# Attention outputs: leaving the output bank by ScalarE, divided by VectorE two heads at a time

## The chip, the cores and the metric

The kernel runs on one core of a Trainium2 chip. The metric is device time in microseconds (us) of one execution. A core has five engines with queues of their own: TensorE (PE in the profile, its weight loads as PEld), VectorE (DVE), ScalarE (ACT), GpSimd (POOL) and SyncE (SP, which here only issues DMAs). Each engine executes its list in order; they wait for one another through semaphores. Matmuls write PSUM, which has 8 banks of 512 fp32 columns in 128 partitions; all else lives in SBUF.

## The reference

One decoder layer over 16 meta tokens and 512 real tokens, width 1024, all in float32:

```
u = rmsnorm(h);  proj = u @ w_in                       # fq fk fv | forget gate | q latent | kv latent | rope key
# group A: 8 heads x 64, logits += cumsum(log f) bias
o_fox = softmax(fq fk^T * scale + bias, causal) @ fv
# group B: 8 heads, q and kv up-projected from latents, 64 + 32 rotary key, 64-wide values
o_mla = softmax(q k^T * scale, causal) @ mv
mix = concat(rmsnorm(o_fox, g_fox_out), rmsnorm(o_mla, g_mla_out));  h = h + mix @ w_o
# hierarchical mixture of experts: 1 of 4 groups, 2 of its 8 experts, 32 experts of 1024 x 256 (w1, w3) and 256 x 1024 (w2)
h = h + sum_e combine_e * (silu(u @ w1_e) * (u @ w3_e)) @ w2_e
```

What matters here is the softmax: each head's output is the product of the exponentials with the values, divided by the sum of the exponentials, for 512 queries.

## The kernel before, in words

The program has one list of instructions per engine. Its stages follow one another: the input projection (until 158 us of the trace), attention of group A (to 228 us), the up-projection of the latents for group B (to 281 us), attention of group B (to 351 us), output projection and router (to about 416 us), then the 32 experts, whose 96 MB of weights stream through four slots of SBUF, and the gathering of their outputs.

Attention keeps the logits transposed, with keys in partitions and the 512 queries in columns. A head g goes through these steps (all in `attend`, once for each group of eight heads):

- `score_maxes(g)` on TensorE (L1707, L1708) computes bf16 logits with queries in partitions into banks 3 to 5; `row_maxes(g)` on VectorE (L1363) reduces them to negated row maxima, four instructions per head. This is done two heads ahead.
- `turn_row(g)` (L1719) transposes the maxima into bank ROW, and ScalarE's `shift_row(g)` (L964) copies them into an extra row of qT, so that the logits come out with the maximum already subtracted.
- `score(g)` (L1731, L1734) puts the fp32 logits into banks 0 to 2; ScalarE's `exp` (L972), three per head, writes the exponentials into probT in SBUF.
- `apply(g)` (L1745) multiplies them with `value(j, h)`, which is 64 columns of values beside 64 columns of ones. So the one bank OUT (bank 6) receives the 64 rows of the output in one half of the partitions (`out_rows`) and the row sums, repeated 64 times, in the other half (`sum_rows`). Even heads have the output in partitions 0 to 63, odd heads in 64 to 127.
- `normalise(g)` on VectorE takes the reciprocal of the 64 x 512 sums out of PSUM (L1369) into sums_r and multiplies it with the output in PSUM (L1370), which gives that head's half of mixT and frees bank OUT. Its semaphore o_done counts heads.

TensorE's list inside the loop over heads is score(g), turn_row(g+1), score_maxes(g+2), apply(g). The last two heads of a group have no score_maxes; in group B one piece of the output projection (`out_project(0, 0, 0)`, L1651) stands in for it in the last but one. apply(g) waits until o_done says that the head before has left bank OUT.

After group A, TensorE waits for o_done of all eight heads and starts the up-projection (L1797): nine units, each with a square on ScalarE (L1002), a sum of squares on VectorE (L1404), a root on ScalarE (L1011), an inverse and scaling on VectorE (L1421), and transposes on TensorE (`turn_up`, L1783). TensorE computes units 0 and 1 and then waits for the staging of unit 0. Ahead of its first unit, VectorE rotates the shared rotary key (L1394 and `rotate`, L1384 to L1389). POOL's `sum_squares` (L715 to L718) squares and adds the chunks of mixT, one for each pair of heads, for the norm of the group; it waits for o_done.

After group B, TensorE does out_project(0, 0, 1), which reads only group A's outputs, and then out_project(0, 1, 0), which waits for o_done of all sixteen heads.

SyncE's list issues the weight DMAs. The first expert's weights (slot 0 of the ring, whose first bytes hold the bf16 copies of q and k) are loaded once the last bf16 logits are computed; expert 1 is loaded before attention, expert 2 near the end of the output projection and expert 3 behind the router. Later experts are loaded as slots come free.

Of the kernel before, what the change touches and what calls it, by code (L numbers as in the profile page):

```python
# [133 lines left out]
def build(nc, a, out, slots=SLOTS):  # L134
# [19 lines left out]
    with ExitStack() as ctx:  # L154
# [107 lines left out]
        probT = [place(f"probT{b}", [P, 3, 512], F32, r_p + 6144 * b) for b in range(2)]  # L262
        sums_r = place("sums_r", [P, SEQ], F32, r_p + 12288)
        assert r_p + 12288 + SEQ * 4 <= r_s + 2 * ST
        scrap = place("scrap", [P, D], F32, r_s)
# [94 lines left out]
        def pair(b, n):  # L360
# [29 lines left out]
        row_turned, row_out = sem("row_turned"), sem("row_out")  # L390
        scored, exped, pv_done, o_done = sem("scored"), sem("exped"), sem("pv_done"), sem("o_done")
        sq_summed, sq_totals, mix_rooted, mix_inv = (sem("sq_summed"), sem("sq_totals"), sem("mix_rooted"),
                                                     sem("mix_inv"))
# [80 lines left out]
        def out_rows(g):  # L474

            return slice(0, HD) if g % 2 == 0 else slice(HD, P)
# [48 lines left out]
        def _(sp):  # L525
# [38 lines left out]

            sp.wait_ge(max_scored, 2 * GS)
            load_expert(0, 0)
# [64 lines left out]
        def _(pool):  # L631
# [75 lines left out]
            def sum_squares(group):  # L707

                c0 = group * DK // 2
                for c in range(c0, c0 + DK // 2):  # L710
                    pool.wait_ge(o_done, 2 * c + 2)
                    if c == c0:
                        if group == 1:
                            pool.wait_ge(mix_rooted, 1)
                        step(pool.tensor_tensor(sq_sum[:, :], mixT[:, c, :], mixT[:, c, :], ALU.mult))  # L715
                    else:
                        step(pool.tensor_tensor(sq_one[:, :], mixT[:, c, :], mixT[:, c, :], ALU.mult))
                        ins = pool.tensor_tensor(sq_sum[:, :], sq_sum[:, :], sq_one[:, :], ALU.add)  # L718
                        if c == c0 + DK // 2 - 1:
                            ins.then_inc(sq_summed, 1)  # L720
                        else:
                            step(ins)
# [96 lines left out]
        def _(act):  # L819
# [137 lines left out]
            def attend(ph):  # L957
# [8 lines left out]
                def exp(g, b):  # L966
# [5 lines left out]
                    act.activation(probT[g % 2][:, b, 0:w], ps[:, b, 0:w], ACT.Exp).then_inc(exped, 1)  # L972

                shift_row(g0)
                for g in range(g0, g0 + H):
                    for b in range(3):
                        exp(g, b)
                    if g + 1 < g0 + H:
                        shift_row(g + 1)

            attend(0)


# [116 lines left out]
        def _(dve):  # L1100
# [256 lines left out]
            def attend(ph):  # L1357
# [7 lines left out]

                def normalise(g):
                    to, by = out_rows(g), sum_rows(g)
                    dve.wait_ge(pv_done, g + 1)
                    step(dve.reciprocal(sums_r[to, :], ps[by, OUT, :]))  # L1369
                    dve.tensor_tensor(mixT[to, g // 2, :], ps[to, OUT, :], sums_r[to, :], ALU.mult  # L1370
                                      ).then_inc(o_done, 1)
# [3 lines left out]
                for g in range(g0, g0 + H):  # L1375
                    if g + 2 < g0 + H:
                        row_maxes(g + 2)
                    normalise(g)

# [163 lines left out]
        def _(pe):  # L1543
# [90 lines left out]
            def out_project(p, group, q):  # L1634
# [3 lines left out]
                pe.wait_ge(wo_scaled, (group + 1) * DK // 2)  # L1638
                pe.wait_ge(o_done, (group + 1) * H)
                if group:  # L1640
# [51 lines left out]
            def attend(ph):  # L1692
# [46 lines left out]
                def apply(g):  # L1739
                    if g > g0:  # L1740
                        pe.wait_ge(o_done, g)
                    for n, (j, b, c0) in enumerate(KEY_BLOCKS):
# [32 lines left out]
            pe.wait_ge(wup_in, 32)  # L1775
            pe.wait_ge(o_done, H)

# [217 lines left out]
```

## Time and profile before

| | us |
|---|---|
| median of 3 runs | 723.79 |
| lowest, highest run | 723.64, 727.7 |
| profiled execution | 727.11 |
| its span in the trace | 725.6 |
| busy in the span: PE, DVE, ACT, POOL | 607.1, 265.2, 190.3, 115.1 |
| VectorE reciprocals of the sums, 16 x 3355 ns | 53.7 |

The span is what the trace shows between the first and the last instruction of the profiled execution; 1.5 us lie around it. All starts below are us from the start of the span. A row of the timeline gives start, duration, engine, line, operation, tiles and shapes, and in brackets how long the engine had been idle before it and what ended the idleness. "x10" is the number of instructions that are merged in a row. The granted clock (PEclk) is the share of 2.4 GHz that TensorE's clock got: 1.00 is 2.4 GHz and 0.50 is 1.2 GHz.

### The profile page before, as it was taken

The page shows a single profiled execution, that of the slowest core. Times are in us where ns is not written, and L with a number is a line of the kernel's source. Part 1 is how long each engine was busy: PE and PEld are TensorE (multiplying, and loading weights), DVE is VectorE, ACT ScalarE, POOL GpSimd, SP SyncE. Part 2 cuts the span into 40 slices and gives each one's busy share as a digit, 9 for nine tenths or more (in the row PEclk, how much of TensorE's full clock was granted, in tenths as well). Part 3 has the DMA queues.
Part 4 walks back from the last instruction along what each step waited for, and adds up shares of the span by engine and source line. Part 5 has one row for each costly group of instructions (what it writes and reads, how often), then busy time and mean ns, then how long its engine had stood idle before and what let it go on. Part 6 is the DMA issues. An engine that isn't in the chain of part 4 may idle for free.

```text
span 725.6 us, 9161 instructions
## 1 busy us (share of the span) xinstructions
PE 607.1 (84%) x3447; PEld 386.3 (53%) x3447; DVE 265.2 (37%) x527; ACT 190.3 (26%) x345; POOL 115.1 (16%) x130
## 2 busy tenths in 40 slices
PE   3699999999996997999999859988788878787740
PEld 2598688885653554665455535544444444444420
DVE  4652324235876475686355521111011111111105
ACT  5532223333321542333144402211111111111110
POOL 8100002110021125811200011111011101111012
PEclk9999899999998998999999969999999999999985
DMA  8900000019200001004000359999999999999948
GB/s 249 374 5 1 1 0 1 1 74 328 87 1 0 1 1 58 1 1 173 1 29 30 147 202 374 382 389 396 397 401 397 403 400 395 394 391 393 402 137 308
DMA packets 39055, 140.17 MB, mean 193 GB/s; under 512 B 8480, under 2 KB 10576, under 8 KB 30576
## 3 DMA queue, kind: packets, MB, share of 16 engines
q1 hardware_dynamic: 29680, 122.83, 44.2%
q0 software_dynamic: 4224, 8.53, 3.8%
q10 hardware_dynamic: 5120, 8.39, 3.2%
q8 instruction: 20, 0.33, 0.2%
q14 instruction: 11, 0.09, 0.0%
HBM read 131.28 MB, written 12.65 MB: 198 GB/s over the span
## 4 chain that ended last, share of the span: by engine, by line
PE 60%; DMA 15%; SPq 9%; DVE 8%; issue 5%; ACT 2%; POOL 1%; ACTq 0%; POOLq 0%; DVEq 0%
PE ps L1612 16%; DMA w<-in_w 10%; PE ps L1889 10%; PE ps L1651 6%; PE ps L1745 6%; PE ps L1731 5%; SPq L588 3%; PE ps L1797 3%; PE ps L1916 3%; SPq L595 3%; DVE sums_r L1369 2%; SPq L589 2%; PE ps L1707 2%; DMA x<-in_x 1%; PE ps L1849 1%
## 5 line engine op out<-in xcount | busy, mean ns | idle before, releaser
L1889 PE MATMUL ps<-w,xt 128*64 128x256 f32 x1024 | 132.7, 417 | 44.9 <-issue 33.4
L1889 PEld LDWEIGHTS ps<-w,xt 128*64 128x64 f32 x1024 | 87.3, 151 | 101.6 <-issue 75.8
L1477 DVE TENSOR_TENSOR xt<-ps,g_ffn_c 128x512 f32<-128x512 f32 x32 | 22.1, 692 | 233.0 <-PE ps L1849 233.0
L765 POOL DMA_INDIRECT xg<-u_rows,idx x32 | 29.8, 932 | 286.1 <-PE ps L1849 216.8
L1369 DVE RECIPROCAL sums_r<-ps 64x512 f32<-64x512 f32 x16 | 53.7, 3355 | 26.8 <-PE ps L1745 26.8
L1916 PE MATMUL ps<-w,hT 128*64 128x512 f32 x256 | 61.8, 604 | 0.0
L1038 ACT ACTIVATE hsb<-ps 128x256 f32<-128x256 f32 x32 | 12.3, 383 | 167.7 <-PE ps L1889 167.7
L1731 PE MATMUL ps<-qT,kT 68*128 68x400 f32 (+9 forms) x160 | 47.9, 424 | 0.0
L1745 PE MATMUL ps<-probT,vals 128*128 128x512 f32 (+4 forms) x160 | 43.4, 416 | 3.5 <-DVE mixT L1370 3.4
L1651 PE MATMUL ps<-w_oa,mixT 128*128 128x512 f32 x96 | 44.5, 599 | 0.9 <-issue 0.8
L972 ACT ACTIVATE probT<-ps 128x416 f32<-128x416 f32 (+1 forms) x48 | 26.1, 544 | 68.8 <-PE ps L1734 68.7
L1745 PEld LDWEIGHTS ps<-probT,vals 128*128 128x128 f32 x160 | 26.7, 190 | 20.1 <-issue 8.1
L1363 DVE TENSOR_REDUCE nmax<-ps 128x1 f32<-128x528 f32 (+1 forms) x64 | 27.9, 496 | 15.6 <-PE ps L1708 15.5
L1056 ACT ACTIVATE yh<-ps 128x512 f32<-128x512 f32 x32 | 19.1, 597 | 53.3 <-PE ps L1916 53.3
L1731 PEld LDWEIGHTS ps<-qT,kT 68*128 68x128 f32 (+1 forms) x160 | 23.6, 191 | 12.1 <-issue 9.1
L1916 PEld LDWEIGHTS ps<-w,hT 128*64 128x64 f32 x256 | 15.6, 136 | 24.0 <-issue 24.0
L1651 PEld LDWEIGHTS ps<-w_oa,mixT 128*128 128x128 f32 x96 | 17.2, 190 | 18.6 <-issue 18.3
L1849 PEld LDWEIGHTS ps<-ident,xg 64*128 64x128 f32 x256 | 18.7, 141 | 15.8 <-issue 15.8
L1849 PE MATMUL ps<-ident,xg 64*128 64x64 f32 x256 | 23.1, 231 | 3.2 <-DMA xg<-u_rows,idx 3.2
L1797 PE MATMUL ps<-w_ukv,ckvT 128*128 128x512 f32 x40 | 20.5, 665 | 4.3 <-DVE mixT L1370 4.3
L698 POOL CAST kTb<-kT 68x1024 bf16<-68x1024 f32 (+1 forms) x5 | 4.8, 966 | 104.4 <-PE ps L1612 92.6
L1576 PE MATMUL ps<-ident,xs 128*128 128x128 f32 (+1 forms) x40 | 8.8, 392 | 14.1 <-DVE xs L1131 14.1
(278 smaller groups left out, 893.0 us busy)
## 6 DMA issues: line engine op xcount, KB each, us to landing
w<-in_w SPq DMA_DIRECT2D x96, 1024.0 KB, 26.4
y_rows<-yh ACTq DMA_DIRECT2D x64, 128.0 KB
w_oa<-in_w_o SPq DMA_DIRECT2D x1, 3072.0 KB, 17.4
x<-in_x SPq DMA_DIRECT2D x4, 512.0 KB, 8.8
w_in_v<-in_w_in SPq DMA_DIRECT2D x1, 2048.0 KB, 11.2
w_in_k<-in_w_in SPq DMA_DIRECT2D x1, 2048.0 KB, 16.2
w_in_q<-in_w_in SPq DMA_DIRECT2D x1, 2048.0 KB, 20.1
u_rows<-u2n SPq DMA_DIRECT2D x4, 512.0 KB, 2.6
```

What stands on the lines that cost most here:

```text
L765: pool.indirect_dma_start(out=xg[e % 2][:, :, :].rearrange("p k n -> p (k n)"), out_offset=None, in_=u2_rows, in_offset=bass.IndirectOffse ...
L972: act.activation(probT[g % 2][:, b, 0:w], ps[:, b, 0:w], ACT.Exp).then_inc(exped, 1)
L1363: dve.tensor_reduce(nmax[g % 2][:, i:i + 1], max_scores(i), X, ALU.max, negate=True).then_inc(maxed, 1)
L1369: step(dve.reciprocal(sums_r[to, :], ps[by, OUT, :]))
L1612: ins = pe.matmul(ps[0:unit_rows(u), n % 4, 0:w], ua[:, k, unit_cols(u)], wa[b][:, k, 0:w], start=(k == 0 and p == 0), stop=(k == DK - 1 a ...
L1651: ins = pe.matmul(ps[:, bank + q, :], mixT[:, k, i * P:(i + 1) * P], wo_chunk(k)[:, q * 512:(q + 1) * 512], start=(k == k0), stop=(k == k0 ...
L1731: pe.matmul(ps[:, b, c0:c0 + wide], kT[0:depth(g), h, block_cols(j)], qT[0:depth(g), h, q0:], start=True, stop=False)
L1745: ins = pe.matmul(ps[:, OUT, q0:SEQ], value(j, g % H), probT[g % 2][:, b, c0:c0 + SEQ - q0], start=(j == 0), stop=(j == 3))
L1797: ins = pe.matmul(ps[0:r, b0 + j, 0:nn], src[:, k, block_cols(t) if kind == "kv" else cols(t)], w[:, k, j * nn:(j + 1) * nn], start=(k == ...
L1849: ins = pe.transpose(ps[:, bank, k * slots:(k + 1) * slots], src[:, k, :], ident[0:slots, 0:slots])
L1889: ins = pe.matmul(ps[j * slots:(j + 1) * slots, 2 + b, 0:F], xt[b][:, k, :], w13[s][:, j, k, :], start=(k == 0), stop=(k == DK - 1))
L1916: ins = pe.matmul(ps[q * slots:(q + 1) * slots, 6 + b, :], hT[b][:, m, :], w2s[s][:, m, q * 512:(q + 1) * 512], start=(m == 0), stop=(m == ...
```

## The change

The outputs leave bank OUT on another engine. Behind the exponentials of head g and the copy of the next head's row, ScalarE runs `copy_output(g)`: it copies the 64 rows of sums into the output's half of a 128 x 512 tile sums_s and the 64 rows of output into mixT. Two heads fill one tile of each. After every odd head, VectorE takes one reciprocal over 128 partitions in place and multiplies mixT with it. o_done now counts pairs and a new semaphore, o_copied, counts the copies, two per head. apply(g) waits for the copies of head g-1, and not for the division; so does the start of the up-projection. There are two tiles sums_s, and they lie in slot 0 of the weight ring; so the load of expert 0 now waits for the last division (`o_done, GS // 2`, with GS = 16).

```diff
@@ -260,8 +260,8 @@
         ST = H * MLA_AUG * 4
         r_s = region(2 * ST)
         probT = [place(f"probT{b}", [P, 3, 512], F32, r_p + 6144 * b) for b in range(2)]
-        sums_r = place("sums_r", [P, SEQ], F32, r_p + 12288)
-        assert r_p + 12288 + SEQ * 4 <= r_s + 2 * ST
+        sums_s = [place(f"sums_s{b}", [P, SEQ], F32, ring + narrow + SEQ * 4 * b) for b in range(2)]
+        assert r_p + 12288 <= r_s + 2 * ST and narrow + 2 * SEQ * 4 <= SLOT
         scrap = place("scrap", [P, D], F32, r_s)
         st_fox = [place(f"st_fox{b}", [P, H, FOX_AUG], F32, r_s + ST * b) for b in range(2)]
         st_lat = [place(f"st_lat{b}", [P, QRK, P], F32, r_s + ST * b) for b in range(2)]
@@ -389,6 +389,7 @@
         narrowed, max_scored, maxed = sem("narrowed"), sem("max_scored"), sem("maxed")
         row_turned, row_out = sem("row_turned"), sem("row_out")
         scored, exped, pv_done, o_done = sem("scored"), sem("exped"), sem("pv_done"), sem("o_done")
+        o_copied, sums_inv = sem("o_copied"), sem("sums_inv")
         sq_summed, sq_totals, mix_rooted, mix_inv = (sem("sq_summed"), sem("sq_totals"), sem("mix_rooted"),
                                                      sem("mix_inv"))
         wo_in = [sem(f"wo_in{b}") for b in range(2)]
@@ -562,7 +563,7 @@
             sp.wait_ge(up_done, NU)
             sp.dma_start(w_ob[:, :, :], w_o_v[:, WO_A:, :]).then_inc(wo_in[1], 16)
 
-            sp.wait_ge(max_scored, 2 * GS)
+            sp.wait_ge(o_done, GS // 2)
             load_expert(0, 0)
 
             for p, i in enumerate(TILE_ORDER):
@@ -708,7 +709,7 @@
 
                 c0 = group * DK // 2
                 for c in range(c0, c0 + DK // 2):
-                    pool.wait_ge(o_done, 2 * c + 2)
+                    pool.wait_ge(o_done, c + 1)
                     if c == c0:
                         if group == 1:
                             pool.wait_ge(mix_rooted, 1)
@@ -971,12 +972,23 @@
                     w = BANK_WIDTH[b]
                     act.activation(probT[g % 2][:, b, 0:w], ps[:, b, 0:w], ACT.Exp).then_inc(exped, 1)
 
+                def copy_output(g):
+
+                    to, by = out_rows(g), sum_rows(g)
+                    act.wait_ge(pv_done, g + 1)
+                    if g >= 4 and g % 2 == 0:
+
+                        act.wait_ge(o_done, g // 2 - 1)
+                    act.activation(sums_s[g // 2 % 2][to, :], ps[by, OUT, :], ACT.Copy).then_inc(o_copied, 1)
+                    act.activation(mixT[to, g // 2, :], ps[to, OUT, :], ACT.Copy).then_inc(o_copied, 1)
+
                 shift_row(g0)
                 for g in range(g0, g0 + H):
                     for b in range(3):
                         exp(g, b)
                     if g + 1 < g0 + H:
                         shift_row(g + 1)
+                    copy_output(g)
 
             attend(0)
 
@@ -1363,11 +1375,12 @@
                         dve.tensor_reduce(nmax[g % 2][:, i:i + 1], max_scores(i), X, ALU.max, negate=True
                                           ).then_inc(maxed, 1)
 
-                def normalise(g):
-                    to, by = out_rows(g), sum_rows(g)
-                    dve.wait_ge(pv_done, g + 1)
-                    step(dve.reciprocal(sums_r[to, :], ps[by, OUT, :]))
-                    dve.tensor_tensor(mixT[to, g // 2, :], ps[to, OUT, :], sums_r[to, :], ALU.mult
+                def normalise(m):
+
+                    dve.wait_ge(o_copied, 4 * (m + 1))
+                    dve.reciprocal(sums_s[m % 2][:, :], sums_s[m % 2][:, :]).then_inc(sums_inv, 1)
+                    dve.wait_ge(sums_inv, m + 1)
+                    dve.tensor_tensor(mixT[:, m, :], mixT[:, m, :], sums_s[m % 2][:, :], ALU.mult
                                       ).then_inc(o_done, 1)
 
                 row_maxes(g0)
@@ -1375,7 +1388,8 @@
                 for g in range(g0, g0 + H):
                     if g + 2 < g0 + H:
                         row_maxes(g + 2)
-                    normalise(g)
+                    if g % 2:
+                        normalise(g // 2)
 
             attend(0)
 
@@ -1636,7 +1650,7 @@
                 i = TILE_ORDER[p]
                 bank = WO_MLA if group else WO_FOX
                 pe.wait_ge(wo_scaled, (group + 1) * DK // 2)
-                pe.wait_ge(o_done, (group + 1) * H)
+                pe.wait_ge(o_done, (group + 1) * H // 2)
                 if group:
 
                     pe.wait_ge(exped, 3 * GS)
@@ -1738,7 +1752,7 @@
 
                 def apply(g):
                     if g > g0:
-                        pe.wait_ge(o_done, g)
+                        pe.wait_ge(o_copied, 2 * g)
                     for n, (j, b, c0) in enumerate(KEY_BLOCKS):
                         pe.wait_ge(exped, 3 * g + b + 1)
                         q0 = first_query(j)
@@ -1773,7 +1787,8 @@
 
 
             pe.wait_ge(wup_in, 32)
-            pe.wait_ge(o_done, H)
+            pe.wait_ge(maxed, NT * H)
+            pe.wait_ge(o_copied, 2 * H)
 
             def turn_up(n):
                 pe.wait_ge(up_staged, n + 1)
```

How the lists of ScalarE and VectorE move is shown by these rows, which give line, operation, output and inputs, shape, and the semaphores that an instruction waits for. First ScalarE, from the first row copy of group A; probT are the exponentials, qT receives the maxima. Before:

```order
L964 ACTIVATE qT<-ps 1x512 [waits row_turned]
L972 ACT_TABLE_LOAD
L972 ACTIVATE probT_126<-ps 128x512 [waits scored]
L972 ACTIVATE probT_126<-ps 128x416 [waits scored] x2
L964 ACTIVATE qT<-ps 1x512 [waits row_turned]
L972 ACTIVATE probT_127<-ps 128x512 [waits scored]
L972 ACTIVATE probT_127<-ps 128x416 [waits scored] x2
```

And now:

```order
L965 ACTIVATE qT<-ps 1x512 [waits row_turned]
L973 ACT_TABLE_LOAD
L973 ACTIVATE probT_126<-ps 128x512 [waits scored]
L973 ACTIVATE probT_126<-ps 128x416 [waits scored] x2
L965 ACTIVATE qT<-ps 1x512 [waits row_turned]
L982 ACTIVATE sums_s_128<-ps 64x512 [waits pv_done]
L983 ACTIVATE mixT<-ps 64x512
L973 ACTIVATE probT_127<-ps 128x512 [waits scored]
L973 ACTIVATE probT_127<-ps 128x416 [waits scored] x2
```

Two copies stand between the row copy of the next head and that head's exponentials; they wait for pv_done, the end of apply(g).

VectorE, from the maxima of head 2 in group A; nmax are the negated maxima. Before:

```order
L1363 TENSOR_REDUCE nmax_176<-ps 128x1 [waits max_scored] x4
L1369 RECIPROCAL sums_r<-ps 64x512 [waits pv_done]
L1370 TENSOR_TENSOR mixT<-ps,sums_r 64x512 [waits dve_step]
L1363 TENSOR_REDUCE nmax_177<-ps 128x1 [waits max_scored] x4
L1369 RECIPROCAL sums_r<-ps 64x512 [waits pv_done]
L1370 TENSOR_TENSOR mixT<-ps,sums_r 64x512 [waits dve_step]
```

And now:

```order
L1375 TENSOR_REDUCE nmax_177<-ps 128x1 [waits max_scored] x4
L1375 TENSOR_REDUCE nmax_178<-ps 128x1 [waits max_scored] x4
L1381 RECIPROCAL sums_s_128<-sums_s_128 128x512 [waits o_copied]
L1383 TENSOR_TENSOR mixT<-mixT,sums_s_128 128x512 [waits sums_inv]
L1375 TENSOR_REDUCE nmax_177<-ps 128x1 [waits max_scored] x4
```

The maxima of two heads run back to back, and then one division serves both; the maxima of the head after the pair stand behind it.

## Rows read from the trace of the kernel before

**Rows 1.** The page: span, and what the DMA engines moved in 40 equal slices

```profile
span 725.6 us, 9161 instructions
...
GB/s 249 374 5 1 1 0 1 1 74 328 87 1 0 1 1 58 1 1 173 1 29 30 147 202 374 382 389 396 397 401 397 403 400 395 394 391 393 402 137 308
```

**Rows 2.** The page's costliest groups: count, busy us, mean ns, idle before

```profile
L1369 DVE RECIPROCAL sums_r<-ps 64x512 f32<-64x512 f32 x16 | 53.7, 3355 | 26.8 <-PE ps L1745 26.8
```

**Rows 3.** Timeline, one period between two apply steps, group A

```profile
180.00 2.72 PE L1745 MATMUL ps<-probT,vals 128*128 128x512 f32 x10
...
182.76 3.35 DVE L1369 RECIPROCAL sums_r<-ps 64x512 f32<-64x512 f32 x1 [1.16 <-PE ps L1745]
...
183.67 0.60 ACT L972 ACTIVATE probT<-ps 128x512 f32<-128x512 f32 x1 [3.80 <-PE ps L1734]
...
186.15 0.69 DVE L1370 TENSOR_TENSOR mixT<-ps,sums_r 64x512 f32<-64x512 f32 x1
...
186.19 0.58 ACT L964 ACTIVATE qT<-ps 1x512 f32<-1x512 f32 x1
...
186.68 0.22 PE L1708 MATMUL ps<-causal,identb 128*128 128x128 bf16 x1
...
186.90 0.19 PEld L1745 LDWEIGHTS ps<-probT,vals 128*128 128x128 f32 x1 [0.19 <-DVE mixT L1370]
```

**Rows 4.** Timeline, apply of the last two heads of group A

```profile
214.48 2.73 PE L1745 MATMUL ps<-probT,vals 128*128 128x512 f32 x10 [0.86 <-DVE mixT L1370]
...
221.37 2.73 PE L1745 MATMUL ps<-probT,vals 128*128 128x512 f32 x10 [1.29 <-DVE mixT L1370]
...
224.13 3.35 DVE L1369 RECIPROCAL sums_r<-ps 64x512 f32<-64x512 f32 x1 [2.82 <-PE ps L1745]
```

**Rows 5.** Timeline, start of the up-projection

```profile
229.55 1.29 POOL L718 TENSOR_TENSOR sq_sum<-sq_sum,sq_one 128x512 f32<-128x512 f32 x1
229.64 1.30 DVE L1386 TENSOR_TENSOR krt<-krg,rope_k 128x80 f32<-128x80 f32 x1
...
230.86 0.23 DVE L1387 TENSOR_TENSOR krt<-krg,rope_k 128x80 f32<-128x80 f32 x1
...
231.28 0.23 DVE L1389 TENSOR_TENSOR krr<-krt 128x80 f32<-128x80 f32 x1
...
235.38 0.69 DVE L1404 TENSOR_REDUCE ss<-sq 128x8 f32<-128x512 f32 x1 [3.87 <-ACT sq L1002]
...
235.87 1.28 ACT L1011 ACT_TABLE_LOAD   x1
...
238.92 1.11 PE L1783 MATMUL ps<-ident,st_mla 128*97 128x128 f32 x8 [0.85 <-DVE st_mla L1421]
```

**Rows 6.** The chain of waits: start, us, engine, line, count

```profile
228.36 6.29 PE ps L1797 x8
...
240.04 3.44 PE ps L1797 x8
...
430.27 5.99 PE ps L1889 x32
```

**Rows 7.** Windows: length; busy us (instructions) of PE, PEld, DVE, ACT, POOL; PEclk; DMA

```profile
162.00:165.00 3.00, 1.29 (x13) 0.81 (x13) 1.90 (x5) 0.00 (x0) 0.00 (x0) 1.00 1.01 423
165.00:168.00 3.00, 3.00 (x18) 1.64 (x17) 1.97 (x6) 0.00 (x0) 0.00 (x0) 0.56 0.79 128
225.00:228.00 3.00, 0.00 (x0) 0.00 (x0) 2.97 (x2) 0.00 (x0) 0.00 (x0) 0.80 0.00 0
```

**Rows 8.** Timeline, end of attention in group B

```profile
350.32 0.69 DVE L1370 TENSOR_TENSOR mixT<-ps,sums_r 64x512 f32<-64x512 f32 x1
...
351.12 1.96 PE L1651 MATMUL ps<-w_oa,mixT 128*128 128x512 f32 x4 [0.79 <-issue]
```

**Rows 9.** Groups by line and shape: count, busy us, mean ns, idle before

```profile
L1110 DVE TENSOR_TENSOR uT_lo<-u_full,uT_hi 128x1024 fp32r<-128x1024 f32 x4 | 4.8, 1211 | 0.0
...
L1412 DVE RECIPROCAL rinv<-root 128x8 f32<-128x8 f32 x9 | 1.8, 203 | 4.1 <-ACT root L1011 4.1
```

## The prediction

> **What bounds the kernel now.** I read the page's DMA slices first. From slice 25 on, that is from about 435 us, the weights of the experts stream at 380 to 400 GB/s until 690 us [rows 1]. That stage is bound by DMA, and nothing in it changes; it starts when attention, output projection and router are done, so an earlier end of attention moves all of it. The question is how much earlier attention ends in each of its two groups.
>
> The old normalisation looks like a large cost: 16 reciprocals of 3355 ns are 53.7 us of VectorE [rows 2]. But a period of a head must be read. apply starts at 180.00, its end releases the reciprocal at 182.76, the multiplication ends at 186.84 (186.15 + 0.69), and the next apply starts at 186.90 [rows 3]. So the chain apply, reciprocal, multiplication, apply closes in 6.90 us. TensorE's own work in this period is almost as long: the last matmul of score_maxes starts at 186.68, 6.68 us after the apply, and the wait for mixT is only 0.19 us [rows 3]. The kernel sits on two limits at once, and taking away the VectorE limit leaves the TensorE one 0.2 us below.
>
> Where there are no score_maxes, the wait is longer: 0.86 us before the seventh apply and 1.29 us before the last [rows 4]. After the last apply nothing covers the normalisation: the reciprocal starts at 224.13 and the up-projection at 228.36 [rows 4, 6].
>
> **Durations of the new instructions.** ScalarE's copy of 64x512 out of PSUM is not in the trace. An exponential of 128x512 takes 0.60 and a one-row copy of 512 takes 0.58 [rows 3]; partitions make no difference there, so a copy is 0.58 and a pair 1.16 at most. Below, the pair can't be under one copy, 0.58; I take 1.16, since both copies have 512 columns. VectorE's reciprocal over 128 partitions: 8 columns over 128 partitions take 203 ns and 512 columns over 64 partitions 3355 ns [rows 2, 9]; the difference over 504 columns is 6.25 ns per column, and 8 of these are 50 of the 203 ns. So columns are paid, not partitions: 3.35 us. The bounds are 3.2 (no PSUM input) and 6.7 (twice 3355, if partitions were paid). The multiplication: 0.69 with one input in PSUM over 512 columns [rows 3], 1.211 for 1024 columns from SBUF [rows 9], whose half is 0.61; I take 0.65.
>
> From the start of the last apply of a pair to the end of its division the old path is 2.76 + 3.35 + 0.04 + 0.69 = 6.84 us; the new one 2.76 + 1.16 + 0.05 + 3.35 + 0.04 + 0.65 = 8.0 us. **A single division is 1.2 us later than before**; bank OUT is free after 3.9 us and not after 6.9.
>
> **Inside a group.** VectorE drops 8 reciprocals of 3.35 in all, but off the path. apply no longer waits: 0.2 us are saved in each of five periods [rows 3], 0.86 and 1.29 before the last two [rows 4]: 3.15 us in group A. In group B the last but one head has a piece of the output projection in the place of score_maxes, so its 0.86 isn't there: 1.0 + 1.29 = 2.3 us.
>
> ScalarE now holds the next head's exponentials behind a wait for pv_done. The copies run from 2.76 to 3.92 us after the start of apply; the first exponential started at 3.67 [rows 3], so it slips by 0.25 us and ends near 4.5, while the next apply can't begin before 6.68. I cost it at nothing; its cover is 2.2 us. The maxima of the head after a pair stand behind a division that ends at 8.0; they start 1.3 us after the next apply instead of with it. What needs them is the row transpose of the following period, behind that apply (2.7 us) and a score step, so this is hidden as well.
>
> **End of group A.** The last apply moves from 221.37 to 218.2. TensorE may start the up-projection after the copies, at 218.2 + 2.76 + 1.16 + 0.05 = 222.2, 6.2 us earlier than 228.36. But VectorE's division ends at 226.2 and then it rotates the key. Before, that rotation ran from 228.2 to 231.5 [rows 5], hidden behind a slow first unit of TensorE; now it ends at 229.5 and the first sum of squares, at 235.38 before, starts there: 5.9 us. TensorE's unit 0 is no limit: it ends at 225.7 at full clock (3.44 us) and at 228.5 at half clock (6.29) [rows 6]. A further 0.8 us goes with the table load of ScalarE: it ran from 235.87 to 237.15 [rows 5], while the sum of squares with its small addition was ready at about 236.3; with squares made earlier, the load is done before. So the first transposes of the up-projection come at 238.92 - 6.7 = 232.2.
>
> In that rotation, one multiplication of 128x80 takes 1.30 us where its twin takes 0.23, and it ends with POOL's addition, which started 0.09 us before it [rows 5]. The Trainium skill, "SBUF — State Buffer", section "Who interferes with whom", says that a VectorE instruction with two SBUF inputs blocks against a GpSimd instruction that reads SBUF, the later one waiting until the earlier is finished. By that rule the stall stays, as POOL's squares still start on the last division; by the row without the stall the rotation would be 1.1 us shorter, VectorE would begin its sums at 228.4 and the gain would be 1.1 larger. The trace agrees with the rule, and the sum keeps 3.3 us.
>
> **The clock is what is taken back.** TensorE finishes units 0 and 1 at 222.2 + 2 x 3.44 = 229.1 and then idles until 232.2, 3.1 us. Before the first attention it was busy 1.29 of 3 us, and the clock fell to half behind that; with no work in 225 to 228 it fell as well [rows 7]. So I expect it to fall in or just behind the new gap. The old fall cost 6.29 - 3.44 = 2.85 us in one unit [rows 6]; the bounds are 0 and 2.85. I take 2.0, nearer to the upper row because the units that follow keep TensorE full and so pay for all of it, but less than it as part of the slow stretch lies in the gap. Group A: 6.7 - 2.0 = 4.7 us.
>
> The Trainium skill, "TensorE: Matmul & The Clock Gate", section "Why this matters for your kernels", also advises against idle gaps between matmul bursts. The fall here is taken from the rows.
>
> **End of group B.** The last division ended at 351.01 [rows 8] and gated out_project(0, 1, 0) at 351.12. It ends 2.3 us earlier by the periods and 1.2 later by the copies: 1.1 us. TensorE's other piece is done earlier and it idles 1.9 us there instead of 0.79.
>
> **The load of expert 0** now waits for that division, which should end at about 345. Its 3 MB need 8 us at 400 GB/s, so they are there by about 353; the first expert matmul is at 430 [rows 6]. The queue behind it holds only the u2 stores, the first of which waits for the output projection. Cost nothing; the cover is over 60 us. The up-projection shares no bank with late copies, as it waits for them.
>
> **Sum.** 4.7 + 1.1 = 5.8 us. Profiled execution 727.11 - 5.8 = 721.3; it was 3.3 us above the median of the three runs, and against that median 723.79 - 5.8 = 718.0.
>
> **The cases.**
>
> - Forecast, the clock falls in the new gap: 718.0. Its own range is 717 to 720, as the fall costs 1 to 2.85 and copies may differ by some tenths. Chance 0.55.
> - The clock stays up. For it: TensorE is fuller around the gap than at 225 to 228, and a gap of 3.1 us is shorter than the old 4.3. Against it: 1.29 of 3 us sufficed for a fall. 2.0 us more: 716.0. Chance 0.22.
> - A new wait takes the place of the old within the heads, so that the five short savings of 0.2 go, in both groups: 2.0 us less, 720.0. The nearest candidate is ScalarE, with 2.2 us of cover. Chance 0.1.
> - The gain is given back, because the expert stream starts no earlier: 723.8. Against it, its start hangs on expert 0's first product [rows 6]. Chance 0.07.
> - **Slower:** the reciprocal pays for partitions and takes 6.7 us. Each group's end is 3.35 us later: group A gains 6.7 - 3.35 - 2.85 (longer gap, the full fall) = 0.5, group B loses 3.35 - 1.1 = 2.25. Together 1.75 slower, 725.5, and more if the maxima behind the division come late. It decides from about 5.8 us per reciprocal on ((5.8 - 0.85) / 2 above 3.35). Against it is the row with 128 partitions [rows 9]. Chance 0.06.
>
> The range of 8 in 10 takes in the first four cases but for the tails: 714.5 to 723.0; the lower end is the warm case with shorter copies and some run-to-run difference. About 1% (7.2 us) is what a measurement of this kernel can tell from no change. The line lies between the forecast and the warm case: faster by over 1% 0.27, within 1% 0.70, slower by over 1% 0.03.
>
> **What would show it.** Apply to apply 6.7 us in the middle of a group, with no wait for mixT; two copies of about 0.58; eight reciprocals of 3.35; up-projection starting about 6 us earlier at full clock, then a gap of 3 us before the first transposes, and PEclk 0.5 in windows behind it; the first output product of group B only 1.1 us less late than the rest. I would be wrong if the exponentials end just before an apply starts, if the reciprocal is far from 3.35, or if the 0.2 us per period don't appear.

## The result and the profile after

| | before | after |
|---|---|---|
| median of 10 runs, us | 725.62 | 719.58 |
| lowest to highest, us | 722.13 to 727.7 | 716.27 to 721.89 |
| profiled execution, us | 727.11 | 718.65 |
| its span, us | 725.6 | 717.2 |

The ratio is 0.9924, with an interval of 0.9902 to 0.9947: 5.5 us faster, 3.8 to 7.1; the medians are 6.0 us apart. The forecast was 5.8 us and 718.0. That is within 1% of no change, the case given most of the chance. One of the ten runs of e7 below took 758.88 us at a mean granted clock of 0.826, and its ratio leaves that run out.

The page of the changed kernel answers to [rows 1, 2]: the DMA slices and the new groups (count, busy us, mean ns, idle before them).

```profile
GB/s 244 382 10 1 1 0 1 1 46 318 130 1 0 1 59 0 1 1 0 206 30 30 192 198 378 383 396 403 401 399 397 400 401 395 397 391 395 393 121 313
...
L1381 DVE RECIPROCAL sums_s<-sums_s 128x512 f32<-128x512 f32 x8 | 26.8, 3352 | 31.4 <-ACT mixT L983 31.4
L982 ACT ACTIVATE sums_s<-ps 64x512 f32<-64x512 f32 x16 | 9.4, 591 | 43.0 <-PE ps L1759 43.0
```

Twice the partitions cost nothing: 3352 ns against 3355. (e1 below has 64 partitions from SBUF, as this one has 128: 3347 ns in the median.) A copy is 591 ns.

The timeline of one period of the changed kernel, group A, answers to [rows 3].

```profile
177.72 2.67 PE L1759 MATMUL ps<-probT,vals 128*128 128x512 f32 x10
...
180.43 0.59 ACT L982 ACTIVATE sums_s<-ps 64x512 f32<-64x512 f32 x1 [2.67 <-PE ps L1759]
181.04 0.59 ACT L983 ACTIVATE mixT<-ps 64x512 f32<-64x512 f32 x1
...
181.66 3.35 DVE L1381 RECIPROCAL sums_s<-sums_s 128x512 f32<-128x512 f32 x1 [2.30 <-ACT mixT L983]
...
184.40 2.67 PE L1759 MATMUL ps<-probT,vals 128*128 128x512 f32 x10
...
185.05 0.69 DVE L1383 TENSOR_TENSOR mixT<-mixT,sums_s 128x512 f32<-128x512 f32 x1
```

The bank is read out at 181.63, 3.9 us after apply began. The next apply comes at 184.40, 6.68 us after the one before and without a wait, while the division is still running.

The end of group A in the changed kernel answers to [rows 4, 5].

```profile
215.61 2.67 PE L1759 MATMUL ps<-probT,vals 128*128 128x512 f32 x10
...
219.56 3.35 DVE L1381 RECIPROCAL sums_s<-sums_s 128x512 f32<-128x512 f32 x1 [7.09 <-ACT mixT L983]
219.67 7.11 PE L1812 MATMUL ps<-w_ukv,ckvT 128*128 128x512 f32 x16 [1.39 <-ACT mixT L983]
...
223.78 1.04 POOL L718 TENSOR_TENSOR sq_one<-mixT 128x512 f32<-128x512 f32 x1 [8.79 <-DVE mixT L1383]
...
223.90 1.01 DVE L1398 TENSOR_TENSOR krt<-krg,rope_k 128x80 f32<-128x80 f32 x1
224.57 1.28 ACT L1023 ACT_TABLE_LOAD   x1
...
224.90 1.29 POOL L719 TENSOR_TENSOR sq_sum<-sq_sum,sq_one 128x512 f32<-128x512 f32 x1
224.99 1.30 DVE L1400 TENSOR_TENSOR krt<-krg,rope_k 128x80 f32<-128x80 f32 x1
...
226.90 0.69 DVE L1418 TENSOR_REDUCE ss<-sq 128x8 f32<-128x512 f32 x1
...
229.55 1.11 PE L1798 MATMUL ps<-ident,st_mla 128*97 128x128 f32 x8 [2.77 <-DVE st_mla L1435]
```

TensorE starts the up-projection at 219.67 during the division, at full clock, and is through two units at 226.78. VectorE is late: division, rotation, first sum at 226.90. Two multiplications of the rotation are long, 1.01 and 1.30 us, and each ends with an operation of POOL. The gap of 2.77 us ahead of the transposes is there; whether the clock fell in it is read from windows (columns as in [rows 7]).

```profile
225.00:228.00 3.00, 1.77 (x5) 0.47 (x3) 2.75 (x7) 0.96 (x2) 1.19 (x1) 1.00 0.00 0
228.00:231.00 3.00, 1.45 (x10) 1.22 (x11) 2.27 (x9) 1.77 (x5) 0.00 (x0) 1.00 0.00 0
...
339.00:342.00 3.00, 1.26 (x2) 0.63 (x3) 2.93 (x4) 0.00 (x0) 1.14 (x2) 0.85 0.23 30
342.00:345.00 3.00, 3.00 (x5) 1.20 (x4) 0.00 (x1) 0.00 (x0) 2.93 (x3) 0.58 0.86 355
```

In this trace it did not fall in group A's gap (PEclk 1.00), but at the end of group B, some 0.4 us after the gap of 338.71 to 340.74 had ended. The chain of waits of the changed kernel shows that end and, last, the first expert product [rows 6].

```profile
332.77 2.51 PE ps L1759 x10
335.28 3.43 PE ps L1665 x8
338.71 2.02 issue
340.74 5.37 PE ps L1665 x8
...
421.70 6.00 PE ps L1904 x32
```

After 2.02 us without work, 8 products take 5.37 us; 8 take 3.43 just before, and the same 8 took 3.67 in the kernel before.

**Where the 8.4 us between the two profiled spans are.** From starts in both timelines, in us:

| stretch | before | after | gained | forecast |
|---|---|---|---|---|
| to the first apply | 173.16 | 171.04 | 2.1 | 0 |
| first to last apply, A | 48.21 | 44.57 | 3.6 | 3.15 |
| last apply to first transposes, A | 17.55 | 13.94 | 3.6 | 3.55, with the fall 1.55 |
| on to the first apply of B | 54.73 | 55.05 | -0.3 | 0 |
| first to last apply, B | 50.53 | 48.01 | 2.5 | 2.3 |
| last apply to out_project(0, 1, 0) | 6.94 | 8.13 | -1.2 | -1.2 |
| on to the first expert product | 79.15 | 80.96 | -1.8 | 0 |
| on to the end | 295.3 | 295.5 | -0.2 | 0 |

The first row isn't the change's. 1.4 of its 2.1 us lie behind the first bf16 logits (162.73 and 161.98), on the same work: in the run of before the clock was down in 165 to 168 [rows 7], in this one it stayed up. The other 0.7 us are there before attention begins. In 80 to 100 us, in the input projection, the clock was down in both runs, longer in the run of before (mean 0.83 and 0.91), and the change touches nothing there. Without the row 6.3 us remain.

### The profile page after: what moved, and what is told of

The parts are those of the page before. It is cut to its first block, busy times and chain, and to the rows that moved or that the text cites. A ratio compares the mean times of both kernels' runs of the same rounds, so it can differ in the third digit from the quotient of the medians.

```text
span 717.2 us, 9183 instructions
## 1 busy us (share of the span) xinstructions
PE 604.3 (84%) x3447; PEld 387.0 (54%) x3447; DVE 232.8 (32%) x511; ACT 208.1 (29%) x377; POOL 114.3 (16%) x130
## 4 chain that ended last, share of the span: by engine, by line
PE 61%; DMA 15%; SPq 9%; DVE 7%; issue 5%; ACT 1%; POOL 1%; ACTq 0%; POOLq 0%; DVEq 0%
PE ps L1626 16%; DMA w<-in_w 11%; PE ps L1904 10%; PE ps L1665 7%; PE ps L1745 6%; PE ps L1759 6%; SPq L589 4%; PE ps L1931 3%; SPq L596 3%; PE ps L1812 3%; SPq L590 2%; PE ps L1721 2%; DMA x<-in_x 1%; PE ps L1864 1%; DMA yg<-y_rows,pos_y 1%
## 5 line engine op out<-in xcount | busy, mean ns | idle before, releaser
L1904 PE MATMUL ps<-w,xt 128*64 128x256 f32 x1024 | 135.6, 424 | 42.3 <-issue 30.2
L1904 PEld LDWEIGHTS ps<-w,xt 128*64 128x64 f32 x1024 | 89.4, 153 | 99.6 <-issue 72.9
L1381 DVE RECIPROCAL sums_s<-sums_s 128x512 f32<-128x512 f32 x8 | 26.8, 3352 | 31.4 <-ACT mixT L983 31.4
L982 ACT ACTIVATE sums_s<-ps 64x512 f32<-64x512 f32 x16 | 9.4, 591 | 43.0 <-PE ps L1759 43.0
```

The source lines that it names most:

```text
L1381: dve.reciprocal(sums_s[m % 2][:, :], sums_s[m % 2][:, :]).then_inc(sums_inv, 1)
L1904: ins = pe.matmul(ps[j * slots:(j + 1) * slots, 2 + b, 0:F], xt[b][:, k, :], w13[s][:, j, k, :], start=(k == 0), stop=(k == DK - 1))
```

## The experiments

Each is an edit of the changed kernel unless it says of the kernel before. Ratios are to the kernel before, timed on the same chip. The changed kernel itself wasn't timed again beside them, so a difference between one of these ratios and its 0.9924 is known to 2.5 to 3 us only; the stretches in the traces are the sharper measure. Where keep_warm appears, matmuls whose results nobody reads are added and nothing is left out.

**Is it the pairing?** e1 divides each head by itself, 16 reciprocals over 64 partitions, ScalarE copying as in the change.

```diff
-                def normalise(m):
...
-                    dve.wait_ge(o_copied, 4 * (m + 1))
-                    dve.reciprocal(sums_s[m % 2][:, :], sums_s[m % 2][:, :]).then_inc(sums_inv, 1)
...
+                def normalise(g):
+                    m, to = g // 2, out_rows(g)
+                    dve.wait_ge(o_copied, 2 * (g + 1))
+                    dve.reciprocal(sums_s[m % 2][to, :], sums_s[m % 2][to, :]).then_inc(sums_inv, 1)
...
```

> The changed kernel, but VectorE divides after every head again, 64 partitions each: 16 reciprocals of 3.35 us and not 8. ScalarE still makes all copies. Theory (what counts is that bank OUT is freed by the copies, and pairing is worth nothing on the path): period in the middle of a group 6.68 us, VectorE's work per head 1.75 + 3.35 + 0.69 = 5.8 us still fits into it; time as the changed kernel, within 1 us. Rival (halving VectorE's work is what pays): period back to 6.9, time back towards the kernel before, some 5 us above the changed kernel.

Measured: 717.37, ratio 0.9881 (0.9848 to 0.9913). The timeline of e1:

```profile
183.08 3.35 DVE L1381 RECIPROCAL sums_s<-sums_s 64x512 f32<-64x512 f32 x1 [0.95 <-ACT mixT L983]
...
185.81 2.67 PE L1758 MATMUL ps<-probT,vals 128*128 128x512 f32 x10
...
189.76 3.35 DVE L1381 RECIPROCAL sums_s<-sums_s 64x512 f32<-64x512 f32 x1 [0.83 <-ACT mixT L983]
```

The period is 189.76 - 183.08 = 6.68 us with twice as many reciprocals, and 14.01 and 8.12 us stand behind the last applies, close to the 13.94 and 8.13 of the change. Halving VectorE's work gives nothing; the copies give all. I had expected e1 within 1 us of the change, and its median is 2 us below. Its trace explains none of that beyond the clock, which didn't fall at the end of B there but did in 162 to 168 us; by the ratios the two are 3.1 us apart, give or take 2.9, so what is left stays open.

**Is it ScalarE?** e10 lets VectorE do the copies.

```diff
+                    dve.tensor_copy(sums_s[g // 2 % 2][to, :], ps[by, OUT, :]).then_inc(o_copied, 1)
+                    dve.tensor_copy(mixT[to, g // 2, :], ps[to, OUT, :]).then_inc(o_copied, 1)
```

> The changed kernel, but VectorE makes the two copies behind each head and not ScalarE. Theory (what matters is that the bank is released by copies that don't wait for a division; VectorE has room, 1.75 + 1.3 + 2.0 = 5.1 of 6.68 us per head): period 6.68 us, time within 1 us of the changed kernel. Rival (the engine matters: the copy of the head behind a pair waits for division and maxima): applies of the heads behind a pair come late, 2 to 6 us slower than the changed kernel.

Measured: 718.03, ratio 0.99 (0.9865 to 0.9934). The timeline of e10:

```profile
189.95 2.67 PE L1756 MATMUL ps<-probT,vals 128*128 128x512 f32 x10
...
192.66 0.68 DVE L1379 COPY sums_s<-ps 64x512 f32<-64x512 f32 x1 [1.06 <-PE ps L1756]
193.38 0.69 DVE L1380 COPY mixT<-ps 64x512 f32<-64x512 f32 x1
194.11 3.35 DVE L1370 RECIPROCAL sums_s<-sums_s 128x512 f32<-128x512 f32 x1
```

Again 6.68 us per period, and the ends are 14.24 and 8.33 us, 0.3 and 0.2 longer than with ScalarE. Which engine copies hardly matters; that the bank is empty before TensorE comes back to it is what counts. At the end of group B the clock fell, as in the change; a window behind the gap of 2.23 us that ends at 340.02:

```profile
340.50:341.00 0.50, 0.50 (x1) 0.00 (x0) 0.50 (x1) 0.00 (x0) 0.50 (x1) 0.50 1.20 164
```

**How long may the division be?** e2 adds a second reciprocal of each pair's sums, into a spare tile.

```diff
+                    dve.reciprocal(spare[:, :], sums_s[m % 2][:, :]).then_inc(sums_inv, 1)
+                    dve.wait_ge(sums_inv, 2 * m + 1)
                     dve.reciprocal(sums_s[m % 2][:, :], sums_s[m % 2][:, :]).then_inc(sums_inv, 1)
```

> The changed kernel with a second reciprocal of 128x512 for each pair, into a spare tile that nothing reads: the rival of the prediction in which a reciprocal costs 6.7 us. Theory: only the ends of the groups lie on the path; group A ends 3.35 us later, plus up to 1 us of clock, group B 3.35 us later, and in the middle the late maxima cost at most 1 us per pair: 6.7 to 11 us slower than the changed kernel, so 1 to 5 us slower than the kernel before. Rival (the division is hidden everywhere): no difference to the changed kernel.

Measured: 731.66, ratio 1.0088 (1.006 to 1.0116). The timeline of e2:

```profile
182.99 2.67 PE L1762 MATMUL ps<-probT,vals 128*128 128x512 f32 x10
183.64 3.35 DVE L1384 RECIPROCAL sums_s<-sums_s 128x512 f32<-128x512 f32 x1
...
187.64 1.74 DVE L1376 TENSOR_REDUCE nmax<-ps 128x1 f32<-128x528 f32 x4
189.44 0.60 PE L1736 MATMUL ps<-ident,nmax 128*1 128x128 f32 x4 [0.89 <-DVE nmax L1376]
...
190.73 1.75 PE L1762 MATMUL ps<-probT,vals 128*128 128x512 f32 x4
```

The maxima are late and the next apply comes after 7.74 us instead of 6.68; four such places are 4.2 us, and both ends are 3.4 us longer (17.32 and 11.51). This is the slower rival's mechanism made real.

**What does the clock take?** e3 fills the two gaps of the change with 11 and 8 matmuls; e4 puts 16 into the kernel before, ahead of its wait for o_done.

```diff
+                if n == 1:
+                    keep_warm(4, 11)
...
+            keep_warm(WO_MLA, 8)
             out_project(0, 1, 0)
```

> The changed kernel with dummy bf16 matmuls in the two gaps that the change opens on TensorE: 11 before the first transposes of the up-projection (gap 2.8 us) and 8 before the first output product of group B (gap 2.0 us). Theory (these gaps let the clock fall in some executions): PEclk stays 1.00 from 215 to 400 us, 0.5 to 2 us faster in the median than the changed kernel. Rival (falls there are rare or hidden): the same within 0.5 us.

```diff
             pe.wait_ge(wup_in, 32)
+            keep_warm(0, 16)
             pe.wait_ge(o_done, H)
```

> The kernel before with 16 dummy bf16 matmuls (3.5 us) ahead of the wait for the last normalisation of group A, where TensorE idled 4.3 us. Theory (part of the gain of the change is that it avoids the fall of the clock there): unit 0 of the up-projection takes 3.4 and not 6.3 us, the first transposes come 2.4 to 3.7 us earlier, time 2.5 to 3.5 us under the kernel before. Rival (the end of the group is bound by VectorE's rotation and the table load, so the clock there is hidden): less than 1 us.

Measured: e3 716.25 (715.57 to 717.34), ratio 0.9872 (0.9847 to 0.9898), some 3 us below the change but only 1.1 below e1 on the same chip, so the matmuls are worth 1 to 3 us; e4 723.29, ratio 0.9961 (0.9934 to 0.9988). The windows of e3 at the two gaps:

```profile
228.00:231.00 3.00, 2.60 (x14) 1.16 (x13) 2.54 (x7) 1.27 (x3) 0.00 (x0) 1.00 0.00 0
...
339.00:342.00 3.00, 2.70 (x11) 1.08 (x10) 2.93 (x4) 0.00 (x1) 0.26 (x1) 1.00 0.00 0
```

That the clock would stay at 1.00 from 215 to 400 us did not come true: it fell in 273 to 282 us, ahead of group B's first apply, where e3 adds nothing.

In the chain of e4 the first unit of the up-projection, 6.29 us in [rows 6], is:

```profile
227.20 3.71 PE ps L1798 x8
```

Its stretch from the last apply to the transposes is 14.88 us, against 17.55 before and 13.94 in the change. So 2.7 of the 3.6 us that the change gained there are the price of the fall, which a filler in the kernel before takes away as well; 0.9 are what the change gives beyond that. In e4's trace the clock fell in another place, in the last apply of group B (2.73 us in the kernel before), so its median shows less than that trace's end of group A:

```profile
341.23 4.41 PE L1745 MATMUL ps<-probT,vals 128*128 128x512 f32 x10 [1.29 <-DVE mixT L1370]
```

**What bounds the end of group A?** e5 rotates the key between the last apply and the last division. e6 also cuts that division into four pieces of 128 columns, between the stagings of the first units.

```diff
+                    if g == H - 1:
+                        rotate_key()
                     if g % 2:
                         normalise(g // 2)
```

> The changed kernel with one edit in VectorE's list: the rotation of the shared key runs between the end of the last apply of group A and the last division, while ScalarE copies, and not behind the division. Theory (VectorE's division plus rotation bounds the first transposes of the up-projection): without POOL's squares beside it the rotation takes about 1.7 us, from 218.3 on in the times of the changed kernel's trace; the division ends near 224, the first sum of squares comes 2.5 to 3 us earlier, and the gap on TensorE shrinks from 2.8 to nearly 0; 2.5 to 3.5 us under the changed kernel. Rival (TensorE's two units or the table load bound it): under 1 us.

```diff
+                if 1 <= n <= 4:
+                    dve.wait_ge(o_copied, 2 * H)
+                    ins = divide_piece(H // 2 - 1, n - 1)
+                    if n == 4:
+                        ins.then_inc(o_done, 1)
                 dve.wait_ge(up_squares, n + 1)
```

> As the run with the rotation first, and the last division of group A is cut into four pieces of 128 columns (about 1 us each), which VectorE does between the stagings of up-projection units 0 to 3: nothing on TensorE needs that division before the output projection. Theory: the first sum of squares now waits for TensorE's unit 0 and ScalarE's square; transposes of unit 0 follow unit 1 without a gap, some 3 us earlier than in the changed kernel, so up to 0.5 us more than with the rotation alone, and the clock cannot fall there: 3 to 4 us under the changed kernel. Rival (pieces delay the staging of units 1 to 4): no gain over the rotation alone, or 1 us lost.

Measured: e5 715.43, ratio 0.9853 (0.9823 to 0.9883); e6 716.33, ratio 0.9867 (0.9837 to 0.9897). The timeline of e5:

```profile
219.26 0.32 DVE L1383 TENSOR_TENSOR krg<-kr,gr_k 128x160 f32<-128x160 f32 x1 [5.86 <-PE ps L1764]
219.93 0.23 DVE L1373 TENSOR_TENSOR krt<-krg,rope_k 128x80 f32<-128x80 f32 x1
...
220.78 3.35 DVE L1400 RECIPROCAL sums_s<-sums_s 128x512 f32<-128x512 f32 x1
...
228.47 1.12 PE L1803 MATMUL ps<-ident,st_mla 128*97 128x128 f32 x8 [0.75 <-DVE st_mla L1440]
```

And of e6:

```profile
225.91 0.69 DVE L1434 TENSOR_REDUCE ss<-sq 128x8 f32<-128x512 f32 x1 [4.28 <-ACT sq L1014]
226.40 1.28 ACT L1023 ACT_TABLE_LOAD   x1
...
229.35 1.11 PE L1814 MATMUL ps<-ident,st_mla 128*97 128x128 f32 x8 [0.75 <-DVE st_mla L1451]
```

In e5 the rotation takes 1.5 us and not 3.3: its multiplications of 1.01 and 1.30 us are 0.24 and 0.23 with POOL idle. The stretch shrinks from 13.94 to 11.92 us. In e6 VectorE is idle before its first sum and the stretch is 11.92 all the same: the next bound, 2.0 us below the first, is TensorE's first unit, then ScalarE's squares with the table load, which no longer hides. Both expectations were too high, 2.5 to 3.5 and some 3 us where the traces give 2.0; for the pieces of e6 it is the rival that came true, no gain over the rotation alone.

**Is the late load of expert 0 free?** e7 is the kernel before with that load behind the last division.

```diff
-            sp.wait_ge(max_scored, 2 * GS)
+            sp.wait_ge(o_done, GS)
```

> The kernel before with only SyncE's wait changed: expert 0 is loaded once all sixteen heads are normalised, not when the last bf16 logits are computed. Theory (the load has over 60 us of cover): as the kernel before, within 1 us. Rival (the late load delays the u2 stores or the first expert): 1 to 8 us slower.

Measured: 726.55, ratio 0.9996 (0.9971 to 1.0022). SyncE's timeline shows the load 26 us later than the 328.10 of before, at no cost:

```profile
354.10 0.34 SPq L539 DMA_DIRECT2D w<-in_w  x1
```

**The clock taken out of both.** e9 is the kernel before with e4's matmuls and more at the start of both groups; e11 is the change with e3's and the same starts. In both traces the granted clock is 1.00 from 150 us to beyond 400.

```diff
                 score_maxes(g0)
+                keep_warm(OUT, 4)
...
+            pe.wait_ge(up_out, NU - 1)
+            keep_warm(OUT, 16)
```

> The kernel before with dummy bf16 matmuls where its clock is seen to fall around attention: 4 between the first two score_maxes of each group, 16 ahead of the wait for the last normalisation of group A, 16 ahead of group B. It and its counterpart of the changed kernel measure what the change gives without the clock. Theory: 2 to 6 us under the kernel before, with a smaller spread of its runs; the changed kernel with dummies lies 5 to 6.5 us under this one (heads 3.5 and 2.45, end of group A 0.9, end of group B -1.2). Rival (half of the change's gain was the clock): the two lie within 3.5 us.

> The changed kernel with dummy matmuls at the same two starts, in the gap before the first transposes and before group B's first output product. Theory: PEclk 1.00 from the first attention to 400 us; 5 to 6.5 us under the kernel before with its dummies, 1 to 3 us under the changed kernel with dummies in its two new gaps alone. Rival: within 3.5 us of the kernel before with its dummies.

Measured: e9 721.96, ratio 0.9946 (0.9917 to 0.9974); e11 715.03, ratio 0.9864 (0.9823 to 0.9905). The medians are 6.9 us apart. By stretches in the two traces: heads of A 3.6, end of A 0.9 (14.87 to 13.94), heads of B 2.5, end of B -1.2. That sums to 5.9 us, what the change is worth with a steady clock. Ahead of the first apply the two traces differ by 1.9 us the other way (169.91 and 171.81), which the change has no part in. The smaller spread that I expected of e9 isn't clear: 6.3 us in 12 runs, against 10.1 in 23 of the kernel before on that chip.

**A better version.** e8 adds to e6: the last division of group B in pieces, whose first releases the first product; sum_totals(1) later; and matmuls at both group starts. e12 moves sum_totals(1) forward again, directly behind the second product of group B.

```diff
+                            ins = divide_piece(H - 1, t)
+                            if n == 0:
+                                ins.then_inc(o_first, 1)
...
-            sum_totals(1)
             out_project(0, 1, 1)
             for p in range(1, NT):
                 out_project(p, 0, 0)
+                if p == 1:
+                    sum_totals(1)
```

> A version that is meant to beat both kernels: the run with the deferred division, and in group B the last division is cut into pieces of 128 columns in the order in which the output projection needs them, so that its first product waits for one piece (1 us) and not for 4 us; the sums of group B's squares are taken one product later; dummy matmuls stand in the gaps at the start of both groups. Theory: 3 to 4 us at the end of group A, 2 us at the end of group B, 1 to 3 us of clock at the starts: 6 to 9 us under the changed kernel, 711 to 713. Rival (the later sums of squares delay the first token tile of the router as much): 3 to 4 us under the changed kernel.

```diff
             out_project(0, 1, 1)
+            sum_totals(1)
             for p in range(1, NT):
                 out_project(p, 0, 0)
-                if p == 1:
-                    sum_totals(1)
```

> The version that beats both kernels, with the sums of group B's squares on TensorE one product earlier, directly behind the second product of group B; its trace had TensorE idle for 1.9 us before the first transposes of the normed tokens, and the clock fell there. Theory: the squares are ready 0.2 us after that product, the idle stretch goes, 1 to 3 us under the version before. Rival (TensorE now waits for the squares): no gain.

Measured: e8 712.31, ratio 0.9815 (0.9784 to 0.9846); e12 710.22 (709.46 to 711.38), ratio 0.9798 (0.9758 to 0.9839). The timeline of e8:

```profile
333.37 0.95 DVE L1382 RECIPROCAL sums_s<-sums_s 128x128 f32<-128x128 f32 x1 [10.53 <-ACT mixT L983]
...
345.66 0.95 PE L1667 MATMUL ps<-ones,sq_sum 128*128 128x1 f32 x8
...
348.50 1.76 PE L1706 MATMUL ps<-ident,x 128*128 128x128 f32 x7 [1.89 <-DVE x L1281]
```

And the chain of e12:

```profile
330.34 2.51 PE ps L1786 x10
332.85 10.30 PE ps L1692 x24
343.15 0.79 PE ps L1667 x8
```

In e8 group B's first product waits no longer for a whole division, but the totals at 345.66 are late for VectorE: TensorE idles 1.89 us and its clock falls at 348.1, within that gap. With the totals earlier TensorE runs on, and the clock stays up. e12 beats both kernels, by about 15 and 9 us; what each of its edits gives wasn't run apart.

## Why the prediction came out right

- **The period.** Right: 6.90 to 6.68 us, five times, with no wait for mixT. The last two saved 1.08 and 1.54 us instead of 0.86 and 1.29, so group A's heads gave 3.6 and not 3.15: the term is too small by 0.2 us in each of the two. The idle time in brackets [rows 4] counts from the end of the matmul before. Where TensorE needn't wait, the next matmul starts before that end: ahead of the last apply, the last matmul of score starts at 219.86 and takes 0.22 us in the kernel before, and the apply comes 1.51 us after its start; in the change it starts at 215.55 with the same 0.22, and the apply 0.06 after. That is 1.45 us and not 1.29. The other 0.1 lies between the start of an apply and the next score step, 2.56 us before and 2.46 now. e1 and e10 show that the copies shorten the period, whoever makes them.
- **Columns, not partitions.** Right: 3352 ns for 128 partitions, 3355 for 64.
- **The new path.** 8.0 us were forecast; the apply starts at 177.72 and the multiplication ends at 185.74, 8.02 us on. ScalarE and the maxima did stay covered. e2 bounds that cover: 3.35 us more break that of the maxima.
- **The end of group A.** Right in size, 3.6 against 3.55, and in what bounds it: VectorE's division and rotation (e5 moves it and gains 2.0 us), then the table load (e6). The rule of the Trainium skill, "SBUF — State Buffer", section "Who interferes with whom", is borne out: 1.30 us beside POOL, 0.23 without. The prediction saw one such stall and priced it at 1.1 us; there are two, each ending with an operation of POOL, the other of 1.01 against 0.24 us, and without both the rotation is 1.8 us shorter (e5). The sum isn't touched, as it kept the whole 3.3 us.
- **The clock.** The size of what is given back was near (2.0 forecast, 1 to 3 by e3 in the median), the place was not. In the traces of the change, e1 and e10, group A's gap of 2.8 to 2.9 us left PEclk at 1.00, three times of three. Group B's gap of 2.0 to 2.2 us, which I had listed and priced at nothing, brought a fall in the change and e10 and none in e1, e5 and e6; in the change it cost 1.7 of the 1.8 us lost behind it (5.37 against 3.67 us for the same 8 products). By these traces two errors, 2.0 us too much in A and up to 1.8 too little behind B, nearly cancel. That they do is luck: the case with the most chance, a fall in the new gap, is not what the trace shows. How often each gap brings a fall in runs without a profile stays open.
- **The starting point.** 718.0 was counted from the median of three runs, 723.79. Over ten runs that median is 725.62, so the gain of 6.0 us ended at 719.58.
- **The rest.** The expert stage took 295.5 us against 295.3, so the shift passed through, and the late load costs nothing (e7). "Given back" and "new wait in the heads" did not occur.
- **The slower rival** was under-priced. I gave 725.5 for a reciprocal of twice the length, "and more if the maxima come late". They do, for 4.2 us, and e2 came out 6.3 us above the kernel before (731.66 and 725.32 on the same chip), where I had priced 1.75.

## What to carry to other kernels

A long operation that reads a shared PSUM bank directly holds the bank for its whole length; a short copy frees it, but the gain ends where the next limit lies, here 0.2 us per period away, and the copy is paid for again wherever nothing covers it, at the end of each phase. Look at these ends for independent work to put ahead of the long operation, and for pieces of it that release their users one by one. Compare short gaps with the granted clock in several traces, and fill them where TensorE has nothing to do: the change's ten runs spread over 5.6 us, the six of e3 over 1.8. The filler may not be alone in that, as six runs of e6 without it spread over 1.9.

## What the runs showed of the hardware

- VectorE's reciprocal takes 3.35 us for 512 float columns over 64 or 128 partitions, from PSUM (before) or SBUF (the change, e1), and 0.95 for 128 columns (e8): it is paid by columns.
- The clock of TensorE isn't set by the length of the last gap alone. It stayed at 2.4 GHz over gaps of 2.77, 2.84 and 2.88 us (the change, e1, e10) and fell to half around ones of 2.02 and 2.23 us (the change, e10) and of 1.89 us (e8). In e4 it fell at about 341.7 us, half a us behind the wait of 1.29 us ahead of the last apply of group B, where no edit was. Such falls cost 1.4 us (before, at the start of group A), 1.7 (the change, e4, e8) and 2.85 (before, at the end of group A).
- Executions differ by where the clock falls, also on work that is the same: the two profiled runs are 2.1 us apart before the first apply, which is ahead of anything that the change touches.
